# The last mixture ended by tiles, z's first product moved ahead of a block's end, and three reads moved one step up

## The reference, cut to what matters

```python
h = modulate(rmsnorm_2(x, norm1_w[1]), shift1, scale1)
z, xbc, dt = split(h @ w_in, [2048, 2048 + 4096])            # state-space layer ("mamba")
xbc = silu(causal_conv4(xbc) + conv_b)                       # x, B and C of 32 heads, 8 groups
dt = softplus(dt + dt_bias);  a = dt * -exp(A_log)
y = gated_scan(xbc, dt, a) + x_heads * D_skip                # needs the running sums of a
g = group_rmsnorm(y * silu(z)) * norm_w
x = x + gate1 * (g @ w_out)
h2 = modulate(rmsnorm_2(x, norm2_w[1]), shift2, scale2)      # mixture of 32 experts, 2 active
hid = silu(h2 @ w1[e]) * (h2 @ w3[e]) * combine[:, e]        # computed for all 32 experts
x = x + gate2 * sum_e(hid[e] @ w2[e])
out = x * rsqrt(mean(x * x) + EPS) * final_norm_w
```

## Time and profile before

| | |
|---|---|
| median of 3 runs | 2306.08 us (2303.16 to 2312.95) |
| the profiled execution | 2303.33 us, of which the span in the trace is 2301.5 us |
| mean granted TensorE clock | 0.924 of full |
| PE busy | 2078.0 us (90%) |
| DVE busy | 1457.0 us (63%) |
| ACT busy | 1041.8 us (45%) |
| moved by DMA | 370.15 MB, mean 161 GB/s |

### The profile page before, as it was taken

How to read it: one execution, slowest core, us unless ns; L and a number is a source line. 1 busy time by engine, 2 the same in 40 slices (tenths; PEclk the granted TensorE clock), 3 DMA queues, 4 the chain that set the end, 5 groups by cost and what they waited for, 6 DMA issues and landing times. The chain is left out here.

```text
span 2301.5 us, 39932 instructions
## 1 busy us (share of the span) xinstructions
PE 2078.0 (90%) x16806; PEld 1971.5 (86%) x16806; DVE 1457.0 (63%) x2365; ACT 1041.8 (45%) x1468; POOL 0.2 (0%) x4
## 2 busy tenths in 40 slices
PE   6978888999989788989998879999979898899997
PEld 6877877999979678779998769999969777899997
DVE  5946555688567655557865666777758655565554
ACT  5643433444465334435444335444455554444443
POOL 0000000000000000000000000000000000000000
PEclk8988888999989888889999889999989988899999
DMA  5322422488543325125975324787724322355552
GB/s 196 121 91 92 156 91 84 143 298 301 185 145 115 98 92 165 65 92 189 323 258 172 126 92 156 269 307 279 280 93 156 123 70 65 126 186 182 181 179 92
DMA packets 101411, 370.15 MB, mean 161 GB/s; under 512 B 11504, under 2 KB 11888, under 8 KB 100976
## 3 DMA queue, kind: packets, MB, share of 16 engines
q1 hardware_dynamic: 99936, 363.38, 47.3%
q10 hardware_dynamic: 1296, 4.21, 0.5%
HBM read 366.50 MB, written 1.05 MB: 160 GB/s over the span
## 5 line engine op out<-in xcount | busy, mean ns | idle before, releaser
L315 DVE TENSOR_TENSOR low<-raw,high 128x1024 fp32r<-128x1024 f32 x590 | 719.2, 1222 | 460.7 <-ACT high L312 458.6
L312 ACT CAST high<-raw 128x1024 fp32r<-128x1024 f32 x590 | 614.0, 1046 | 552.4 <-PE ps L380 487.2
L378 PE MATMUL ps<-hh,high 128*128 128x256 f32 x2832 | 826.8, 292 | 39.3 <-DVE hl L697 28.6
L379 PE MATMUL ps<-hh,low 128*128 128x256 f32 x2832 | 809.6, 286 | 0.0
L380 PE MATMUL ps<-hl,high 128*128 128x256 f32 x2832 | 808.7, 286 | 0.0
L378 PEld LDWEIGHTS ps<-hh,high 128*128 128x128 f32 x2832 | 558.4, 197 | 61.4 <-issue 50.8
L379 PEld LDWEIGHTS ps<-hh,low 128*128 128x128 f32 x2832 | 555.7, 196 | 0.5 <-issue 0.5
L380 PEld LDWEIGHTS ps<-hl,high 128*128 128x128 f32 x2832 | 554.6, 196 | 0.0
L378 PE MATMUL ps<-ffn_high,high 128*128 128x256 f32 x672 | 193.2, 287 | 10.3 <-PEq L1926 5.8
L379 PE MATMUL ps<-ffn_high,low 128*128 128x256 f32 x672 | 190.6, 284 | 0.0
L380 PE MATMUL ps<-ffn_low,high 128*128 128x256 f32 x672 | 190.6, 284 | 0.0
(11 more groups left out here) (450 smaller groups left out, 2777.8 us busy)
## 6 DMA issues: line engine op xcount, KB each, us to landing
raw<-in_stream SPq DMA_DIRECT2D x590, 512.0 KB, 4.0
ada_rows<-in_ada SPq DMA_DIRECT2D x96, 512.0 KB, 5.5
c_act<-in_c SPq DMA_DIRECT2D x3, 512.0 KB, 4.2
bias<-in_bias ACTq DMA_DIRECT2D x1, 1536.0 KB, 7.4
xT<-in_xT SPq DMA_DIRECT2D x4, 256.0 KB, 5.9
out<-xT SPq DMA_DIRECT2D x1, 1024.0 KB, 3.8
par<-in_par ACTq DMA_DIRECT2D x1, 842.0 KB, 9.1
hybrid_const<-in_const ACTq DMA_DIRECT2D x1, 800.0 KB, 6.0
```

What stands on the lines that cost most here:

```text
L312: return act.copy(self.high[:, slot, :], self.raw[:, slot, :])
L315: return dve.tensor_tensor(self.low[:, slot, :], self.raw[:, slot, :], self.high[:, slot, :].bitcast(F32), ALU.subtract)
L378: pe.matmul(out, sh, mh, start=start, stop=False, **more)
L379: pe.matmul(out, sl, mh, start=False, stop=False, **more)
```

## The change

Three edits.

1. In `mamba`'s block one, `keep_sums` stands after pair 2 on DVE and no longer after pair 3. `rest_of_sums` stays after pair 3.
2. z's pair 0 (48 matmuls) moves from block two, where it stood behind the first decay sums, to the end of block one on PE. It waits until PSUM bank 0 has been read for pair 12, the last pair of xbc in that bank. ACT's rounding of z's unit 4 (`wz.scalar(act, 0)`) moves to block one with it, between the rounding for pair 15 and its SiLU. DVE's part of that unit stays in block two.
3. In the last mixture the downs of experts 28 to 31 are reordered: PE waits once for all hidden halves, and then does, for each pair c of output tiles, all four experts (24 matmuls), so that the first tiles are complete before the last. DVE adds each pair of tiles as it is complete, ACT squares it, and PE adds the squares of pair c - 1 behind the matmuls of pair c, into bank 2 in place of bank 4. The final norm stands in the same block, its square root's table is loaded by a small activation ahead of it, and `out` is stored by four transfers of 256 KB, each as soon as its two tiles are scaled.

```diff
@@ mamba, block one, tensor
+                    prod.after_read(pe, max(j for j in range(KX // 2) if prod.pairs[j][0] == prod_z.pairs[0][0]))
+                    for m in range(2):
+                        prod_z.tensor(pe, h, 0, only=m)
@@ mamba, block one, vector
-                        if j == 3:
+                        if j == 2:
                             keep_sums()
                         if j == 3:
                             rest_of_sums()
@@ mamba, block one, scalar
                         w.scalar(act, 2 * j + 1)
+                        if j == KX // 2 - 1:
+                            wz.scalar(act, 0)
                         prod.after_read(act, j)
@@ mamba, block two, tensor
                     running_sum(1)
-                    prod_z.tensor(pe, h, 0, only=0)
-                    prod_z.tensor(pe, h, 0, only=1)
@@ mamba, block two, scalar
                         if hd == 1:
-                            wz.scalar(act, 0)
                             wz.scalar(act, 1)
@@ mixture, sync
+                    if last:
+                        for c in range(KD // 2):
+                            sp.wait_ge(out_scaled.sem, out_scaled.base + c + 1)
+                            sp.dma_start(out[:, 2 * c:2 * c + 2, :], xT[:, 2 * c:2 * c + 2, :]).then_inc(stored, 16)
...
@@ mixture, tensor (by_tile = range(28, 32) where last)
-                        if s >= LAG:
+                        if s >= LAG and s - LAG not in by_tile:
                             down(s - LAG)
...
+                        pe.wait_ge(hidden_done.sem, hidden_done.base + E_N // 2)
+                        for c in range(KD // 2):
+                            for j in by_tile:
+                                halves = w.arrived(pe, down_at(j))
...
+                                for m in (2 * c, 2 * c + 1):
+                                    ins = three_products(...)
...
+                            if c < KD // 2 - 1:
+                                tell(ins, tiles_done)
+                            if c:
+                                add_squares(pe, c - 1, bank=2)
+                        tell(add_squares(pe, KD // 2 - 1, bank=2), final_summed)
@@ mixture, scalar
+                    if last:
+                        act.activation(stat[:, 3, 0:1], ones[:, 0:1], ACT.Sqrt)
+                        act.wait_ge(variance.sem, variance.base + 2)
+                        tell(act.activation(stat[:, 1, :], stat[:, 0, :], ACT.Sqrt), deviation)
@@ mixture, vector
-                    dve.wait_ge(*w.done(3 * E_N - 1))
+                    if not last:
+                        dve.wait_ge(*w.done(3 * E_N - 1))
                     for m in range(KD):
+                        if last and m == KD - 2:
+                            dve.wait_ge(*w.done(3 * E_N - 1))
+                        elif last and m % 2 == 0:
+                            dve.wait_ge(tiles_done.sem, tiles_done.base + m // 2 + 1)
...
+                    if last:
+                        done = InOrder(dve, dve_step)
+                        dve.wait_ge(final_summed.sem, final_summed.base + 1)
+                        tell(dve.tensor_scalar(stat[:, 0, :], ps[:, 2, 0:T], 1.0 / D, EPS, ALU.mult, ALU.add), variance)
+                        dve.wait_ge(deviation.sem, deviation.base + 2)
+                        done(dve.reciprocal(stat[:, 2, :], stat[:, 1, :]))
+                        for k in range(KD):
+                            ins = dve.scalar_tensor_tensor(xT[:, k, :], xT[:, k, :], P2("final")[:, k:k + 1], stat[:, 2, :],
+                                                           ALU.mult, ALU.mult)
+                            if k % 2:
+                                tell(ins, out_scaled)
@@ the program's end
-        mixture(1, Norm(mgain[:, 3, :], shift(1, 1), hT))
-        rms_norm(P2("final"))
-        with new_block() as block:
-            ...
-                sp.dma_start(out, xT[:, :, :]).then_inc(stored, 16)
+        mixture(1, Norm(mgain[:, 3, :], shift(1, 1), hT), last=True)
```

More of the change, by code:

```diff
@@ L612, in square_tiles, with add_squares @@
             tell(act.activation(sq[:, 2 * c:2 * c + 2, :], xT[:, 2 * c:2 * c + 2, :], ACT.Square), squares)
-        def add_squares(pe, c, turn=0):
+        def add_squares(pe, c, turn=0, bank=4):
             pe.wait_ge(squares.sem, squares.base + turn * KD // 2 + c + 1)
             for k in (2 * c, 2 * c + 1):
-                pe.matmul(ps[:, 4, 0:T], ones, sq[:, k, :], start=(k == 0), stop=(k == KD - 1))
+                ins = pe.matmul(ps[:, bank, 0:T], ones, sq[:, k, :], start=(k == 0), stop=(k == KD - 1))
+            return ins
         gained_squares = signal("gained_squares")
@@ L2451, in route, with mixture @@
             tell(dve.tensor_copy(combine[:, :, E_N:2 * E_N], combine[:, :, 0:E_N]), combine_ready)
-        def mixture(l, norm):
+        def mixture(l, norm, last=False):
             w = ring.claim(3 * E_N)
@@ L2472, in mixture @@
             mods = Modulation(DEPTH, ADA, ADA, moe) if l == 0 else None
+            by_tile = range(E_N - RING, E_N) if last else ()
             def rows(i):
@@ L3084, in hybrid_and_moe @@
         mamba(Norm(mgain[:, 2, :], shift(1, 0), hT))
-        mixture(1, Norm(mgain[:, 3, :], shift(1, 1), hT))
-        rms_norm(P2("final"))
-        with new_block() as block:
-            @block.sync
-            def _(sp):
-                sp.dma_start(out, xT[:, :, :]).then_inc(stored, 16)
-                sp.wait_ge(stored, 16)
+        mixture(1, Norm(mgain[:, 3, :], shift(1, 1), hT), last=True)
 def kernel(x, norm1_g, w_in, hg_lb, hg_norm_g, gla_w2, gla_b, gla_norm_g, cmp_pos_k, cmp_pos_v,
```

28 lines of the change are left out of this document (12 added, 16 removed).

## The result

| | before | changed |
|---|---|---|
| median | 2304.91 us (2300.98 to 2312.95, 8 runs) | 2288.36 us (2281.19 to 2294.14, 8 runs) |
| ratio | 1 | 0.9925, 95% interval 0.9908 to 0.9942 |
| profiled execution | 2303.33 us, span 2301.5 | 2281.19 us, span 2279.4 |
| mean granted clock | 0.924 | 0.938 |

The change makes the kernel faster by 0.75%, about 17 us (by the interval, 13 to 21). The two profiled executions lie 22.1 us apart. The profiled one of the changed kernel is the lowest of its eight, so part of that is chance: its first `a` product, ahead of all that is changed, starts 3.0 us earlier (1711.46 against 1714.42).

A forecast was written before the change was run, and what follows sets the result against it. It took TensorE, busy 90% of the span, as the bound, with gains only in its waits and the half clock after them. From 2303.33 us, - 7.1 - 7.3 + 0.4 = - 14.0 gave 2289.3; forecast 2290, range 2284 to 2299.

The forecast's parts named there:

- Edit 1, -7.1: Block one: earlier reads of the sums start pair 4's taps 7.1 us sooner; bounds 5.0 to 7.9.
- Rival (a): Block one: early reads hide, TensorE only waits later; gain 0, time 2296.5 us; 13%.
- Edit 2, -7.3: Block seam: z's pair 0 fills the wait; 7.6 us gained in block two less 0.3 at the seam.
- Edit 3, +0.4: Kernel's end: new 3.1 us wait and half clock outweigh the smaller store; 0.4 us lost net.
- its clock term: Last mixture: the 3.1 us wait drops the clock, and the start at half clock costs 1.5 us.
- the geometric mean: Last store, 256 KB instead of 1024: lands in 1.9 us, taken between 0.95 and 3.8.
- (b): Block two and the end: clock falls at both; block two gains 4.2 - 0.3, end loses 3.5; 2295.8 us; 17%.
- (c): Final norm: the moved table load is late and the square root waits for it, 1.28 us; time 2291; 10%.
- (d): Block two: without dense z first, clock stays half for the stage; slower, 2324 us with W = 35; 4%.

The follow-up runs named there:

- e1_reads: The kernel before with only keep_sums moved behind pair 2: 2299.54 us median of 12, ratio 0.9960 to the kernel before.
- e10_changed_again: The changed kernel, unaltered, in a second profiled execution: 2290.06 us median of 6, ratio 0.9929 to the kernel before.
- e4_two: The changed kernel with only experts 30 and 31 done by tiles, not four experts: ratio 0.9911 to the kernel before.
- e9_two_again: The changed kernel with only experts 30 and 31 done by tiles, run in a second session: ratio 0.9903 to the kernel before.
- e2_z: The kernel before with only z's pair 0 and the rounding of unit 4 moved to block one's end: 2298.37 us median of 12, ratio 0.9950.
- e8_split: e4_two with each group's sixteen one-column variance products placed in the middle of z's half product: 2290.38 us median of 6, ratio 0.9931 to the kernel before.
- e3_tail: The kernel before with only the changed last mixture, norm and stores: 2309.11 us median of 12, ratio 0.9996 to the kernel before.
- e6_turn: The changed kernel with the four transposes of x and VectorE's scaling of them one pair later: ratio 0.9936 to the kernel before.
- e7_both: The changed kernel with the transposes and scaling one pair later and only experts 30 and 31 by tiles: ratio 0.9943 to the kernel before.

## Why the prediction was right

**Edit 1, -7.1: right.** The transposes start 0.16 us after the reads end (foretold 0.15), the wait is 2.2 us (foretold 2.3), and with the clock held pair 4's taps come 6.39 and 6.57 us after pair 3's (foretold 6.5), that is 7.2 and 7.1 sooner. Where the clock falls it is 5.6, within the bounds. VectorE was to be just in time for these taps; it waits 0.15 us for ScalarE's copy in e1_reads and 0.35 in e10_changed_again. Rival (a), that the early reads hide, is refuted by e1_reads alone, whose ratio excludes 1.

**Edit 2, -7.3: the mechanism right, the size 1.1 too large.** Foretold was z's pair 1 at 4.65 us behind the start with the clock held, and 2.8 + 2.45 + 1.6 = 6.9 with the clock fallen. It came at 5.34 in three of eight executions with z moved (changed, e4_two, e9_two_again) and at 7.14 to 8.56 in five. I chose the value near the full clock, because TensorE comes from 5.7 us of dense work. That reason is not borne out: the clock fell in most. Both values came later than foretold, by 0.7 and by 0.2 to 1.7, and at full clock the rows show why: I let the path go over VectorE's weights of the second head, but they were ready 0.93 us before TensorE came to them, for TensorE does the next two heads' sums and the first head's output ahead. At the seam 0.3 us were to be lost; by the loop's column it is nothing in e2_z (69.6), and beside edit 1 between nothing and 0.2 (70.0 to 70.2 against 70.0). At equal half-clock time the stage gained 6.2.

**What was not in the sum.** The means over the table are 129.8 us for block two in the five executions of the old order, at a mean clock of 0.884, and 120.5 in the seven of the new (e8_split left out), at 0.915. That is 9.3 less: the 6.2 of the line, and 3.1 for half-clock time that was 30.1 us in the mean and is 20.6. The prediction had no term for the clock behind the block's start. The old order showed 0.86 in three of five, the new one in one of seven. Whether the move itself makes the falls rarer, or this is chance among so few, stays open: between 20 and 100 us of the stage the mean clock was 0.91, 0.98, 0.91, 1.00, 0.91 in the old order and 1.00, 1.00, 0.94, 0.98, 0.98, 1.00, 0.98 in the new (both in the table's order), so either can be free of falls and either can have them.

**Edit 3, +0.4: the mechanism right, and its clock term seen once in four.** Foretold and measured: wait 3.1 and 3.00; from the end of the last hidden half to the last tile 13.2 without a fall, 13.0 in e10_changed_again; the variance 2.7 us after that, 2.8; the last store's issue 5.9 after the variance, 6.0 (2270.94 to 2276.9); and 2.5 us from there to the end where it was 4.2, so 1.7 gained by the smaller store against the 1.9 of the geometric mean. The 1.5 us of fallen clock came in the changed kernel's first execution (26.5 us of tail, 0.6 lost) and not in its second, nor in e3_tail and e6_turn (24.9, 1.0 gained, where the sum without its clock term has 1.1).

**Rivals (b), (c), (d).** (b) asked for a fall at both places: of the changed kernel's two executions each shows one of them, and with it 17.1 or 18.5 us of reads, so the time does not come near 2295.8. Nor did block two gain as little as its 4.2: in the five executions with a fall at the start z's pair 1 still came 4.7 to 6.1 us sooner. (c), the late table: the load of 1.28 us starts 0.02 us after the last square, and the small activation starts 0.01 after the load. The Trainium skill (ScalarE: Activation LUTs, What ACT_TABLE_LOAD costs) has a drain of about 1380 ns beside the load; this trace does not show one, and the measurement decides. The square root waits for the variance, not for the table. (d), half clock for the whole stage: block two's clock was 0.86 at the least, no less than in the kernel before. (a)'s time in the prediction, 2296.5, should read 2296.4; nothing hangs on it.

**The sum.** Stage means of the runs with and without each edit: reads 24.6 to 17.3 (-7.3, e6_turn and e7_both left out), loop 69.7 to 70.1 (+0.4), block two -9.3, tail between -1.0 and +0.6. Together -15.6 to -17.2. The two timings of the changed kernel give (1 - 0.9925) x 2304.9 = 17.3 and (1 - 0.9929) x 2304.2 = 16.4. Forecast were 14.0. The missing 2 to 3 us are of the size of the 3.1 that block two's clock gave; with edit 2 at its 6.2 the stages would come to 12.5 to 14.1. So the sum was near because its parts were, and its errors (edit 2 too large by 1.1, the clock left out, the tail's fall that mostly did not come) partly cancelled: that part is luck. The edits taken alone give 9.2, 11.5 and 0.9 us by their ratios, 21.6 in all, with intervals of some 4 to 5 us on each, so that the timings leave room for an overlap of theirs and do not prove one.

## What to carry to other kernels

A wait is best filled with work that needs nothing new: 48 matmuls that stood behind the seam of two blocks fit in its 6.3 us of waiting and returned 6 to 7, while the same move inside the block returned nothing. When the order is changed so that results come out earlier, look at what must now be complete first: four experts by tiles made a wait of 3.0 us, two made none, and the tail with two was 2.4 us shorter than with four. And when TensorE's clock goes up and down by itself, compare stages at the same granted clock before you credit a change: two executions of one kernel were 8.2 us apart in one stage.

## What the runs showed of the hardware

The length of TensorE's wait does not settle whether the clock falls. A wait of 2.2 us was followed by a fall in one execution and by none in the five others with it (the column reads: 18.5 against 16.9 to 17.1); one of 3.0 us by a fall in one and by none in three (the tail: 26.5 against 24.9). And in block two it fell with no wait at all. Windows of the kernel before:

```profile
1850.00:1860.00 10.00, 10.00 (x60) 7.49 (x59) 5.35 (x10) 5.92 (x10) 0.00 (x0) 0.93 0.17 54
1860.00:1870.00 10.00, 10.00 (x46) 7.71 (x45) 4.20 (x10) 4.55 (x11) 0.00 (x0) 0.73 0.18 54
```

TensorE shows as busy in all of both, with 60 and 46 matmuls, the heads' small ones among them, and the clock is 0.93 and 0.73. The Trainium skill (TensorE: Matmul & The Clock Gate, What's actually happening) says that the unit which sets the clock looks at TensorE by a beat of its own, which does not start with the kernel. The runs are in keeping with this, since the same instructions with waits equal to 0.02 us met different clocks; the beat itself no run here shows.

A microsecond at half clock costs a mixed stage less than it costs matmuls alone. In block two each us at half clock made the stage 0.32 us longer, by both lines. Matmuls back to back would lose some 0.43, an estimate from their starts, 0.12 us apart at full clock and 0.21 at half. A likely reason, not tested, is that ScalarE and VectorE set part of the stage's time.
